# A block of mixers and 32 experts on one core: rows and results of the experts turned by VectorE, expert weights stored by ring slot

## What is computed

```python
def expert_block(args):
    xb, e = args
    hgu = xb @ w_gate_up[e] + b_gate_up[e]
    gate, up = jnp.split(hgu, 2, axis=-1)
    gate = jnp.minimum(gate, SWIGLU_LIMIT)
    up = jnp.clip(up, -SWIGLU_LIMIT, SWIGLU_LIMIT)
    act = (up + 1.0) * gate * jax.nn.sigmoid(SWIGLU_ALPHA * gate)
    return act @ w_down[e] + b_down[e]
```

## Time and profile before

| What | Value |
|---|---|
| Median of 3 executions | 2565.97 us (2565.05 to 2567.79) |
| Profiled execution: span | 2562.3 us |
| Outside the span, against the median | 3.7 us |
| TensorE busy | 2497.7 us, 97% of the span |
| VectorE, ScalarE, GpSimd busy | 1032.2, 617.9 and 212.9 us |
| First product of pass 0 to the end of the last | 806.4 to 2413.9 us |
| Moved by DMA | 528.6 MB, 206 GB/s over the span |

### The profile page before, as it was taken

The page is one execution under the profiler, slowest core; times in us unless marked ns, Lnnn a source line. Parts: engine busy times, 40 slices in busy tenths (PEclk is TensorE's granted clock), DMA queues, the critical chain, the costliest instruction groups (busy, mean ns, idle before and its releaser), DMA issues. The chain is left out here.

```text
span 2562.3 us, 51308 instructions
## 1 busy us (share of the span) xinstructions
PE 2497.7 (97%) x20593; PEld 2270.5 (89%) x20594; DVE 1032.2 (40%) x1894; ACT 617.9 (24%) x1358; POOL 212.9 (8%) x227
## 2 busy tenths in 40 slices
PE   8999999999998999999999999999999999999898
PEld 6787877797446999999999999999999999999776
DVE  4667618725225222223223332334323323232386
ACT  4434323643111111111111111111111111111265
POOL 0000115352000000000000000000000000000130
PEclk9999997999998999999999999999999999999899
DMA  4111220001715766777888888999999999999562
GB/s 150 40 49 58 91 74 19 18 4 35 262 59 180 260 216 227 239 241 258 274 261 274 277 287 285 298 299 288 303 308 301 307 299 303 309 306 307 192 220 75
DMA packets 438616, 528.58 MB, mean 206 GB/s; under 512 B 11892, under 2 KB 407112, under 8 KB 438472
## 3 DMA queue, kind: packets, MB, share of 16 engines
q1 hardware_dynamic: 425672, 481.08, 57.1%
q0 software_dynamic: 12800, 45.36, 5.9%
HBM read 485.77 MB, written 40.63 MB: 205 GB/s over the span
## 5 line engine op out<-in xcount | busy, mean ns | idle before, releaser
L1852 PE MATMUL ex_psum<-ex_xT,weight_ring_a 128*128 128x134 f32 (+14 forms) x7168 | 895.4, 286 | 0.8 <-ACT ex_xT L1838 0.8
L1852 PEld LDWEIGHTS ex_psum<-ex_xT,weight_ring_a 128*128 128x128 f32 x7168 | 883.2, 191 | 1.0 <-issue 1.0
L1892 PE MATMUL ex_psum<-ex_hT,weight_ring_b 128*128 128x134 f32 (+14 forms) x4096 | 521.7, 286 | 0.0
L1892 PEld LDWEIGHTS ex_psum<-ex_hT,weight_ring_b 128*128 128x128 f32 x4096 | 508.2, 191 | 0.0
L1862 DVE TENSOR_SCALAR ex_gate<-ex_psum,bias_gate_up 128x192 f32<-128x192 f32 x256 | 95.0, 413 | 665.5 <-PE ex_psum L1852 665.3
L1866 DVE TENSOR_SCALAR ex_up<-ex_psum,bias_gate_up 128x192 f32<-128x192 f32 x256 | 95.0, 413 | 401.0 <-PE ex_psum L1852 401.0
L1879 ACT ACTIVATE ex_sig<-ex_gate 128x384 f32<-128x384 f32 x128 | 66.9, 523 | 777.0 <-DVE ex_gate L1862 776.8
L1900 ACT ACTIVATE ex_yT<-ex_psum,bias_down 128x192 f32<-128x192 f32 x256 | 93.6, 416 | 522.0 <-PE ex_psum L1892 522.0
L2188 PE MATMUL project_psum<-n_hi,w_in_hi 128*128 128x512 f32 x464 | 187.0, 403 | 2.9 <-DVE n_lo L507 2.9
L2188 PE MATMUL project_psum<-n_hi,w_in_lo 128*128 128x512 f32 x464 | 181.8, 392 | 0.0
L2188 PE MATMUL project_psum<-n_lo,w_in_hi 128*128 128x512 f32 x464 | 181.6, 391 | 0.0
(11 more groups left out here) (350 smaller groups left out, 2741.3 us busy)
## 6 DMA issues: line engine op xcount, KB each, us to landing
weight_ring_a<-in_w_gate_up SPq DMA_DIRECT2D x224, 1024.0 KB, 5.6
weight_ring_b<-in_w_down SPq DMA_DIRECT2D x128, 1024.0 KB, 5.6
weight_ring_b<-in_w_gate_up SPq DMA_DIRECT2D x32, 1024.0 KB, 5.2
y_dram<-ex_y_a SPq DMA_DIRECT2D x33, 512.0 KB, 4.6
w_in_pieces<-in_w_in SPq DMA_DIRECT2D x29, 512.0 KB, 3.7
y_dram<-ex_y_b SPq DMA_DIRECT2D x20, 256.0 KB, 3.7
project_work<-in_x SPq DMA_DIRECT2D x8, 512.0 KB, 6.8
gates_dram<-project_work POOLq DMA_DIRECT2D x16, 256.0 KB, 2.9
```

What stands on the lines that cost most here:

```text
L1852: mm = pe.matmul(self.ps[:, bank, i * CAP:i * CAP + width], w[:, k, i * P:(i + 1) * P], self.xT[:, k, 0:width], start=(k == 0), stop=(k == ...
L1892: mm = pe.matmul(self.ps[:, bank, i * CAP:i * CAP + width], w[:, k, i * P:(i + 1) * P], self.hT[:, k, 0:width], start=(k == 0 and i == 0), ...
```

## The change

**Weights.** The host stores `w_gate_up` and `w_down` in pieces, one for each ring slot, so that each partition of a slot is one run of 8 KB (`weight_pieces`). The input features are dealt out differently: partition p of k tile j holds feature 8p + j, where it held 128j + p. The same holds for the output features of `w_down`. A down slot now holds two k tiles with all eight output tiles, so that chunk c of `pe_down` takes two k tiles and adds to all eight output tiles; these lie in banks 4, 5, 6 and in the rest of bank 7, whose first 14 columns stay with the lists.

**Rows and results.** A row of 1024 numbers is gathered as four pieces of 256, which land on four different partitions: piece a of token s of a block of 32 on partition 32a + s. So there are six indirect transfers for a wide list and four for a narrow one. The list of tokens is spread (`dve_spread`), summed by a small product (`pe_fold`) and completed (`dve_list`), to give each partition its piece's address. VectorE then turns all 32 x 32 squares of the rows in one instruction (`dve_turn_x`) and those of the results in another (`dve_turn_y`); TensorE's turns, ScalarE's copies of them and VectorE's are gone. ScalarE moves out all eight tiles of a pass behind its last chunk. The results are stored by four transfers of 1 KB runs each instead of one or two of 4 KB. In `route` the bias of the down product is loaded and turned in another layout (eight turns of 32 rows for two of 128).

The core of the diff:

```diff
+    pieces, at = (g.w_gate_up, i) if i < 8 else (g.w_down, i - 8)
+    return pieces[e, at].rearrange("p (k n) -> p k n", k=slot_tiles(i))
+def slot_tiles(i):
+    return KT if i < 8 else 2
+    gu = w_gate_up[0].reshape(E, P, KT, 2, 4, 256).transpose(0, 4, 3, 1, 2, 5).reshape(E, 8, P, KT * 256)
+    down = w_down[0].reshape(E, 4, 2, P, P, KT).transpose(0, 1, 3, 2, 5, 4).reshape(E, 4, P, 2 * D)
...
-    DOWN = (4, 5)
-    TURN, LIST = 6, 7
+    DOWN = [(4, 0), (4, CAP), (5, 0), (5, CAP), (6, 0), (6, CAP), (7, P), (7, P + CAP)]
+    SPARE, LIST = 6, 7
...
+        self.rows = sb("rows", [P, BLOCKS, PIECE])
+        self.y = sb("y", [P, BLOCKS, PIECE])
...
+        pool.wait_ge(self.listed, x + 1)
+        pool.wait_ge(self.x_turned, x).then_inc(self.rows_free, 1)
+        for b in range(BLOCKS_NARROW if narrow else BLOCKS):
+            pool.indirect_dma_start(out=self.rows[:, b, :], out_offset=None, in_=self.g.xn_dram.rearrange("t (a n) -> (t a) n", a=QUARTERS),
+                                    in_offset=bass.IndirectOffsetOnAxis(ap=self.list[:, b:b + 1], axis=0)).then_inc(self.rows_in, 16)
...
+    def dve_spread(self, dve, x, narrow=False):
-        dve.wait_ge(self.rows_in[0], 16 * x)
+        dve.wait_ge(self.folded, x)
+        block = self.g.k[:, K_BLOCK:K_BLOCK + BLOCKS_NARROW]
+        dve.tensor_tensor(self.spread_a[:], block.unsqueeze(1).to_broadcast([P, 2, BLOCKS_NARROW]),
...
+    def pe_fold(self, pe, x, narrow=False):
+        pe.wait_ge(self.listed, x)
+        for v in range(2):
+            mm = pe.matmul(self.ps[:, self.LIST, 8:8 + BLOCKS_NARROW], self.fold[:], self.spread_a[:, v], start=(v == 0), stop=(v == 1))
+        for v in range(0 if narrow else 2):
+            mm = pe.matmul(self.ps[:, self.LIST, 8 + BLOCKS_NARROW:8 + BLOCKS], self.fold[0:CAP - P, :], self.spread_b[:, v], start=(v == 0), stop=(v == 1))
+        mm.then_inc(self.folded, 1)
...
+    def dve_list(self, dve, x, landed, narrow=False):
+        dve.wait_ge(self.folded, x + 1)
+            dve.tensor_scalar(self.list[:, 0:n], self.ps[:, self.LIST, 8:8 + n], quarter, None, ALU.add).then_inc(self.listed, 1)
...
+    def dve_turn_x(self, dve, x, landed, after, narrow=False):
+        n = BLOCKS_NARROW if narrow else BLOCKS
+        dve.wait_ge(self.rows_in, landed)
+        dve.wait_ge(self.gu_done, after)
+        dve.transpose(self.xT[:, :, 0:n * SQ].rearrange("p j (b s) -> p j b s", s=SQ),
+                      self.rows[:, 0:n, :].rearrange("p b (r j) -> p j b r", r=SQ)).then_inc(self.x_turned, 1)
...
     def pe_down(self, pe, m, c, width):
-        w = ring_slot(self.g, 8 + c).rearrange("p (k n) -> p k n", k=KT)
-        bank = self.DOWN[c % 2]
+        w = ring_slot(self.g, 8 + c).rearrange("p (k j q) -> p k j q", k=2, j=KT)
         pe.wait_ge(self.g.w_in_ring[8 + c], 16 * m + 16)
-        pe.wait_ge(self.yT_kept, 8 * m + 2 * c + 2)
-        for k in range(KT):
-            if c == 0 and k % 2 == 0:
-                pe.wait_ge(self.h_done, 4 * m + k // 2 + 1)
-            for i in range(2):
-                mm = pe.matmul(self.ps[:, bank, i * CAP:i * CAP + width], w[:, k, i * P:(i + 1) * P], self.hT[:, k, 0:width],
-                               start=(k == 0 and i == 0), stop=(k == KT - 1), skip_group_check=True)
+        if c == 0:
+            pe.wait_ge(self.yT_kept, 8 * m + 4)
+            pe.wait_ge(self.listed, m + 2)
+        pe.wait_ge(self.h_done, 4 * m + c + 1)
+        for i in range(2):
+            k = 2 * c + i
+            for j, (bank, first) in enumerate(self.DOWN):
+                mm = pe.matmul(self.ps[:, bank, first:first + width], w[:, i, j], self.hT[:, k, 0:width],
+                               start=(k == 0 and j % 2 == 0), stop=(k == KT - 1), skip_group_check=True)
         mm.then_inc(self.dn_done, 1)
...
+    def act_down(self, act, m, e):
+        act.wait_ge(self.dn_done, 4 * m + 4)
+        act.wait_ge(self.y_turned, m + 1)
+        for j in (6, 7, 0, 1, 2, 3, 4, 5):
+            bank, first = self.DOWN[j]
+            bias = self.g.b_dn[:, bass.ds(e, 1), j:j + 1].rearrange("p a b -> p (a b)")
+            act.activation(self.yT[:, j, :], self.ps[:, bank, first:first + CAP], ACT.Identity, bias=bias).then_inc(self.yT_kept, 1)
...
+    def dve_turn_y(self, dve, y, narrow=False):
+        n = BLOCKS_NARROW if narrow else BLOCKS
+        dve.wait_ge(self.yT_kept, 8 * y + 4)
+        dve.wait_ge(self.y_out, 16 * QUARTERS * y + 16)
+        dve.transpose(self.y[:, 0:n, :].rearrange("p b (r j) -> p b j r", r=SQ),
+                      self.yT[:, :, 0:n * SQ].rearrange("p j (b s) -> p b j s", s=SQ)).then_inc(self.y_turned, 1)
...
+    def store(self, sp, y, region, narrow=False):
+        n = BLOCKS_NARROW if narrow else BLOCKS
+        sp.wait_ge(self.y_turned, y + 1)
+        for a in range(QUARTERS):
+            sp.dma_start(region[0:n * SQ, a * PIECE:(a + 1) * PIECE].rearrange("(b s) r -> s b r", s=SQ),
+                         self.y[a * SQ:(a + 1) * SQ, 0:n, :]).then_inc(self.y_out, 16)
...
+            pieces, at = (g.w_gate_up, i) if i < 8 else (g.w_down, i - 8)
+            src = pieces[bass.ds(e, 1), at].rearrange("a p n -> (a p) n").rearrange("p (k n) -> p k n", k=slot_tiles(i))
+            sp.dma_start(ring_slot(g, i).rearrange("p (k n) -> p k n", k=slot_tiles(i)), src).then_inc(g.w_in_ring[i], 16)
...
+            pool.memset(x.y[:], 0.0).then_inc(x.y_zero, 1)
+            pool.memset(x.yT[:], 0.0).then_inc(x.yT_kept, 4)
+            x.gather(pool, 0)
...
+            keep_running(pe, x.ps[:, x.SPARE, :], g.k, 1)
+            pe.wait_ge(x.ready, 2)
+            x.pe_list(pe, 0, 4)
+            x.pe_fold(pe, 0)
+            keep_running(pe, x.ps[:, x.SPARE, :], g.k, 8)
+            def one_pass(e, width, narrow_x):
                 for c in range(4):
-                    x.pe_gate_up(pe, e, 8 * e + 4, c, width)
+                    x.pe_gate_up(pe, e, e + 1, c, width)
                     if c == 0:
-                        x.pe_list(pe, e + 1, narrow_x)
-                    x.pe_turn_y(pe, 8 * e + 4, 8 * e + 4, c, narrow_y)
-                for c, turns in DOWN_THEN_TURNS:
+                        x.pe_list(pe, e + 1, 8 * e + 4, narrow_x)
+                    if c == 1:
+                        x.pe_fold(pe, e + 1, narrow_x)
+                for c in range(4):
                     x.pe_down(pe, e, c, width)
-                    for q in turns:
-                        x.pe_turn_x(pe, e + 1, 8 * e + 8, q, narrow_x)
...
+            dve.memset(x.list[:], 0).then_inc(x.act_step, 2)
+            dve.tensor_copy(x.fold[:], g.k[:, K_FOLD:K_FOLD + P]).then_inc(x.ready, 1)
             x.dve_find(dve, 0, 0)
-            x.dve_list(dve, 0)
-            dve.memset(x.y_a[:, 0:1], 0.0).then_inc(x.y_out[0], 16)
-            dve.memset(x.ps[:, 0:6, :], 0.0).then_inc(x.gu_kept, 8)
+            x.dve_spread(dve, 0)
+            x.dve_list(dve, 0, None)
+            dve.memset(x.ps[:, x.LIST, P:P + 2 * CAP], 0.0).then_inc(x.gu_kept, 4)
+            dve.memset(x.ps[:, 0:6, :], 0.0).then_inc(x.gu_kept, 4)
+            x.dve_turn_x(dve, 0, x.rows_total(0, False), 0)
             x.dve_order(dve)
...
                         if c == 0:
-                            x.dve_list(dve, e + 1, first + 1 >= NARROW)
-                        x.dve_keep_y(dve, e, 8 * e + 4, c, first - 1 >= NARROW)
-            for q in range(4):
-                x.dve_keep_y(dve, E, 8 * E + 4, q, narrow=True)
+                            x.dve_spread(dve, e + 1, narrow)
+                        if c == 1:
+                            x.dve_list(dve, e + 1, x.rows_total(e, first >= NARROW), narrow)
+                        if c == 2:
+                            x.dve_turn_y(dve, e, first - 1 >= NARROW)
+                    x.dve_turn_x(dve, e + 1, x.rows_total(e + 1, narrow), 8 * e + 8, narrow)
+            x.dve_turn_y(dve, E, narrow=True)
```

More of the change, by code:

```diff
@@ L1378, in route @@
         b_router = sb("b_router", [P, E])
-        rows = xnT[:, 0:6]
+        rows = xnT[:, 0:4]
+        down_rows = ring_slot(g, 7)[0:E, D:2 * D]
         stat = sb("stat", [P, 3, NT])
@@ L1442, in turn_biases @@
                 pe.wait_ge(rows_in, 32)
-                for q in range(6):
-                    mm = pe.transpose(ps[:, 6 + q // 4, (q % 4) * P:(q % 4 + 1) * P], rows[:, q], ident)
+                for q in range(4):
+                    pe.transpose(ps[:, 6, q * P:(q + 1) * P], rows[:, q], ident)
+                for j in range(KT):
+                    mm = pe.transpose(ps[:, 7, j * E:(j + 1) * E], down_rows.rearrange("e (c j) -> e j c", j=KT)[:, j], ident[0:E, 0:E])
                 mm.then_inc(b_turned, 1)
@@ L1729, in dve_list @@
         if not narrow:
[L1730 to L1737 removed]
+            n, more = CAP - P, BLOCKS - BLOCKS_NARROW
@@ L1997, in _ @@
                         if i == 7:
-                            x.store(sp, 8 * e + 4, *rows(e), narrow=first > NARROW)
+                            x.store(sp, e, rows(e), narrow=first > NARROW)
```

(5 more changed lines are left out.)

252 lines of the change are left out of this document (83 added, 169 removed).

## The result

The changed kernel takes 2504.57 us (median of 4 runs, 2502.6 to 2506.34) against 2566.27 (4 runs, 2565.05 to 2567.79) on the same chip: ratio 0.9758, 95% interval 0.9744 to 0.9772. The forecast was 2498.9 with a range of 2486 to 2514. The time came out 5.7 us longer, and it was composed differently.

A forecast was written before the change was run, and what follows sets the result against it. TensorE's instructions were taken to bound the experts stage. The terms -89.8 + 4.3 + 12.5 + 4.0 + 1.9 = -67.1 us give span 2495.2; with 3.7 from span to median, 2498.9 us, range 2486 to 2514 for 8 in 10.

The forecast's parts named there:

- 816 turns go: Experts stage: TensorE's 816 turns vanish at 0.11 us each, the distance between starts; 89.8 us less.
- fold: Experts stage: 100 small TensorE products added, at 0.043 us each; 4.3 us more, between 0 and twice that.
- start: Start of experts stage: expert order queued behind VectorE's first turn delays expert 1's list product; 12.5 us more (8 to 20.4).
- clock behind the wait: After TensorE's wait in pass 0: clock at 0.50 for 8 us, half of them lost; 4.0 us more (0 to 8).
- end: Behind the last chunk: eight evictions, turn and four store issues delay the next stage; 1.9 us more, 7 with dear turn.
- routing stage: Route stage ahead of the experts: changes only by a few small turns; taken as 0.
- VectorE's turn: Rows and results: 1.28 us narrow, 1.93 wide, hidden within passes; rival of a dear turn (6.55, 9.8): 2512 us, chance 0.08.
- The gathers' lockout: Rival's possible reason: VectorE's two-port mode locks out GpSimd's issues, so gathers run one after another; 2629 us, chance 0.06.
- Transfers: Rival: weight transfers take the bound, so narrow passes stay at 44.8 us and lose 21.7 us; 2521 us, chance 0.06.

The follow-up runs named there:

- pe_turns_24: Changed kernel with 24 TensorE turns of a constant added in each of the 32 passes, ahead of the first down product: 2590.2 us, ratio 1.0089.
- order_split: Changed kernel with VectorE's turn of the first rows moved into the middle of the sorting of the experts: 2499.09 us, ratio 0.9747.
- late_and_split: Changed kernel with order_split's edit and the bias turn, with its copies, moved behind the second tile's projection: 2496.77 us, ratio 0.9725.
- turns_2: Changed kernel with each VectorE turn of rows and results inside the loop done twice: 2508.08 us, ratio 0.9766.
- before_8k: Kernel before the change with only the expert weights stored in pieces, so transfers read 8 KB runs: 2564.27 us, ratio 0.9994.
- gathers_serial: Changed kernel with GpSimd, inside the loop, waiting for each gathered block to land before issuing the next: 2626.88 us, ratio 1.0252.

## Why the prediction came out as it did

The forecast's span was 2495.2, the measured one 2503.6. By its own steps:

| step | predicted | measured | read from |
|---|---|---|---|
| 816 turns go | -89.8 | -88.9 | 0.109 each, pe_turns_24 |
| fold | +4.3 | +10.1 | passes: 18 x 0.39 + 14 x 0.22 |
| start | +12.5 | +11.6 | timeline |
| clock behind the wait | +4.0 | +2.5 | order_split |
| end | +1.9 | +0.6 | timeline |
| routing stage | 0 | +4.3 | timeline, late_and_split |
| stages before it | 0 | +1.5 | varies by itself |

The rows sum to -58.3; the spans differ by 58.7. The row of the fold is what the passes shortened too little, so it holds whatever else is new in them. The span was missed by 8.4 us and the time by only 5.7, because the 3.7 us from span to median were 1.0 here. Each execution on record takes 1.7 to 1.8 us more than its own span; what lies beyond that depends on which run was profiled, so this part of the closeness is luck.

*The turns* were right, and that the price is the distance of starts and not the mean of 275 ns. *The fold was mis-sized*: I took the list's 0.043 for a product "between 0 and twice that". A product costs 0.025. What I left out is paid by the float32 products around it: with the turns gone, 64 gate products behind the list take 7.21 us instead of 7.14, and 96 behind the fold 10.78 instead of 10.71. Before, a turn stood behind the list. A wide pass shortens by 3.10 us and a narrow one by 1.52 where 32 and 16 turns are 3.49 and 1.74. The rows of a narrow pass close: its 16 turns took 1.77 us in their places, and what came in is 0.06 for the fold, 0.07 for each of these two runs of products, and 0.05 in all for the list and the products behind. That the first weights behind products of two or four columns are loaded in the open would fit this; it was only argued.

*The start* held in its mechanism: the order of the experts, queued behind the turn, set the end of the wait, as order_split shows. Two sizes were off and nearly cancelled. The sixth gather had landed 2.75 us behind its issue instead of 4.4, and the turn took 2.92 instead of 1.93.

*VectorE's turn* was priced like a plain operation, 1.28 and 1.93 us. It takes 2.03 and 2.96, a fixed part and about 1.8 ns for each number of a partition. The Trainium skill ("VectorE: DVE Perf Modes", The three transpose paths) had led to an estimate of 2.5 us for the narrow one, 0.5 too much where mine was 0.75 too little. In the passes it changed nothing (turns_2).

*The clock* was right in kind, 0.50 behind the wait, but for 5.2 us, not 8. *The end* was shorter because eight evictions took 2.60 us (2.9) and the first product of the next stage came 4.8 us behind the first store's issue, where I had counted 1.2 to the last of four issues and 5.3 from there; the turn, 2.02 for 1.28, took 0.7 of this back.

*The routing stage* is the step that failed: "The route stage changes by a few small turns; I take 0." I counted the instructions and not the transfer in front of them. `b_down` now goes to 32 partitions in 4 KB pieces. It was issued as early as before, 12.6 us into the stage for 12.7, but landed 8.7 us behind its issue for 6.8 (7.1 in before_8k, so the larger weight runs are not the cause). The bias turn, one instruction stream behind 14 us of projection, came 2.05 us later for it, and in this profile the clock took nearly as much again. The trace of before had the warning in it: TensorE already waited 0.35 us there.

*The rivals.* The gathers' lockout did not come: 170 issues, 969 ns each on average, where the earlier trace rows has 1.05 and 0.92. The Trainium skill's rule ("SBUF — State Buffer", SBUF: two separate sides) had no case in the narrow pass, whose four issues were over before VectorE's first turn began. Where issues and turns did meet, the longest took 1.27 us in the changed kernel, and in gathers_serial issues within a turn took 0.95, so these turns locked nobody out. Transfers never took the bound: 316 GB/s at a share of 0.90, and with old runs 0.98.

## What to carry over

A wait on an engine that sets the time costs its length and can cost the lower clock behind it, here 1.8 us behind 2.4 and 2.5 behind 6.1. Whether a wait of 1 to 2 us does so changed from run to run: one of 1.24 us cost as much clock as 2.40, and in three other runs 1.5 to 1.9 cost none. With the wait removed (late_and_split) the clock stayed at 1.00. Look at every wait of a few tenths that stands in front of an edited transfer, also outside the stage that the change is about. And price a small group among large products by the distance between the large ones on both sides, not by its own products.
